# One stage for the sample rows' delta rule, paged attention and head gate, with the heads' split moved into the MLP stage

## What is computed

```
proj = rmsnorm(x) @ w_in
o_g  = gated delta rule(q, k, v, g, beta, S0)      # 4 heads, state S of 128 x 128 per head and sequence
o_g  = rmsnorm(o_g) * silu(z)                      # per head
o_d  = (softmax(q1 k1) - lam * softmax(q2 k2)) @ v # 4 heads; samples read 512 past keys and values from pages
o_d  = rmsnorm(o_d) * (1 - lam_init)
h    = x + concat(o_g, o_d) @ w_out
y    = h + (silu(u_gate) * u_value) @ w_down,  u = causal conv(rmsnorm(h) @ w_up)
```

## Time and profile before

| | us |
|---|---|
| median of 3 runs | 1882.63 (1879.61 to 1882.79) |
| the profiled execution | 1877.6 |
| its span, first to last instruction | 1876.0 |
| stages one and two of the span | 780.9 |
| `delta_sample` | 62.6 |
| `attention_sample` | 71.9 |
| `head_gate` | 66.6 |
| `output_and_mlp` | 894.0 |

### The profile page before, as it was taken

One profiled execution on the slowest core, in us unless ns is written; L12 is line 12 of the kernel. 1 busy time (PEld: TensorE's weight loads), 2 busy tenths in 40 slices (PEclk: granted clock), 3 DMA queues, 4 the chain that ended last, 5 costly groups with the idle time before them and its releaser, 6 DMA issues. The chain is left out here.

```text
span 1876.0 us, 28466 instructions
## 1 busy us (share of the span) xinstructions
PE 1722.7 (92%) x11078; PEld 1615.1 (86%) x11078; DVE 1007.0 (54%) x1450; ACT 536.0 (29%) x803; POOL 247.1 (13%) x434
## 2 busy tenths in 40 slices
PE   5999999997999999765559999999999999999998
PEld 5999998895888888644139999999999999999997
DVE  4444388673556665332163455555655655655654
ACT  4243323321434443201232223212212212212213
POOL 3100022214333333104000000000000000000000
PEclk9999999997999999857769999999999999999999
DMA  4311111221000000119302121101101101101103
GB/s 142 119 45 48 45 36 42 84 81 35 1 12 1 12 1 1 51 45 359 140 10 66 48 68 57 57 22 56 56 22 56 56 22 56 56 22 56 55 0 102
DMA packets 114550, 105.29 MB, mean 56 GB/s; under 512 B 5387, under 2 KB 104221, under 8 KB 112022
## 3 DMA queue, kind: packets, MB, share of 16 engines
q1 hardware_dynamic: 111666, 93.35, 16.0%
q0 software_dynamic: 1536, 8.39, 1.1%
q10 hardware_dynamic: 1270, 2.48, 0.4%
HBM read 86.13 MB, written 18.07 MB: 56 GB/s over the span
## 5 line engine op out<-in xcount | busy, mean ns | idle before, releaser
L2656 PE MATMUL f_up<-h_hi,w_hi 128*128 128x352 f32 x1032 | 335.1, 325 | 1.9 <-DVE w_lo L2465 1.2
L2656 PE MATMUL f_up<-h_hi,w_lo 128*128 128x352 f32 x1032 | 333.4, 323 | 0.0
L2656 PE MATMUL f_up<-h_lo,w_hi 128*128 128x352 f32 x1032 | 333.4, 323 | 0.0
L179 PE MATMUL proj<-x_hi,win_hi 128*128 128x352 f32 x672 | 227.4, 338 | 5.3 <-issue 3.0
L179 PE MATMUL proj<-x_hi,win_lo 128*128 128x352 f32 x672 | 217.5, 324 | 0.0
L179 PE MATMUL proj<-x_lo,win_hi 128*128 128x352 f32 x672 | 217.3, 323 | 0.0
L2656 PEld LDWEIGHTS f_up<-h_hi,w_hi 128*128 128x128 f32 x1032 | 193.8, 188 | 2.5 <-DVE w_lo L2465 1.5
L2656 PEld LDWEIGHTS f_up<-h_hi,w_lo 128*128 128x128 f32 x1032 | 194.1, 188 | 0.0
L2656 PEld LDWEIGHTS f_up<-h_lo,w_hi 128*128 128x128 f32 x1032 | 193.7, 188 | 0.0
L2663 PE MATMUL f_down<-f_g_hi,dn_hi 128*128 128x352 f32 x512 | 165.4, 323 | 0.0
L2663 PE MATMUL f_down<-f_g_hi,dn_lo 128*128 128x352 f32 x512 | 164.7, 322 | 0.0
(11 more groups left out here) (405 smaller groups left out, 3033.9 us busy)
## 6 DMA issues: line engine op xcount, KB each, us to landing
w_raw<-in_w_up SPq DMA_DIRECT2D x44, 512.0 KB, 3.9
win_raw<-in_w_in SPq DMA_DIRECT2D x28, 512.0 KB, 4.0
dn_raw<-in_w_down SPq DMA_DIRECT2D x11, 1024.0 KB, 5.1
p_key<-in_cache_k SPq DMA_DIRECT2D x32, 256.0 KB, 6.4
p_val<-in_cache_v POOLq DMA_DIRECT2D x32, 256.0 KB, 6.2
x_scratch<-feat SPq DMA_DIRECT2D x1, 4224.0 KB, 13.4
feat<-x_scratch SPq DMA_DIRECT2D x1, 4224.0 KB, 17.4
feat<-in_x_prompt SPq DMA_DIRECT2D x8, 512.0 KB, 8.4
```

What stands on the lines that cost most here:

```text
L179: mm = nc.tensor.matmul(out, w[:, k, :], x[:, k, g * TG:(g + 1) * TG], start=(k == 0 and i == 0), stop=(k == KT - 1 and i == 2))
L2656: mm = nc.tensor.matmul(up[u % RING][:, 0:TG], a[s][:, kk, :], b, start=(kk + x == 0), stop=(kk == KT - 1 and x == 2))
```

## The change

The three stages become one, `sample_stage`, with one barrier where there were three.

- The delta rule's steps are laid between the steps of the key loop. PE's order in the loop is: `delta_join(0)`, turn 1, `delta_extend(0)`, score 0; `delta_join(1)`, turn 2, `delta_extend(1)`, score 1; `delta_solve`, turn 3, `delta_state` (the 64 matmuls), score 2; the new values, turn 4, the output, score 3; then in b = 4 and b = 5 four state updates each, two ahead of the turn and two behind it; then b = 6 and 7 as before.
- The transposed keys go through two banks in place of four, one head each: ACT keeps heads 0 and 2, DVE heads 1 and 3. The other banks are `bank_a` and `bank_b` (delta rule, state updates, later the sums of squares), two for scores and two for the fresh part; the score and key banks also serve the first delta steps.
- The state update is cut into eight halves of one 512-column matmul each. The decay of the state moves from DVE to POOL, four instructions behind POOL's value loads.
- Values of sequences 0 to 3, 6 and 7 lie in tiles of `feat`. Those of 6 and 7 take the place of 0 and 1, and are loaded only when `multiply(0)` is done.
- z is read on SP's queue behind the keys of b = 2, silu is applied by ACT at b = 5. The sums of squares go group by group: `sum_heads(0)` behind the loop, `sum_heads(1)` behind `turn_map(1)` and `turn_out(0)`, `sum_heads(2)` behind `multiply(1)`. Roots, reciprocals and spreading work on one column group at a time (and a small fourth group of the 32 sample columns); the spread results use the two key banks in turn. The multiplication with silu(z) moves to POOL.
- The split of the heads into `o_hi` and `o_lo` moves into `output_and_mlp`, ahead of and around the split of the first weights. x is read there as well (8 DMAs on SP's queue, behind the first two weight loads). The first output tile is computed with the heads in the outer loop and the three column groups in the inner one.

The diff, cut to its core (NV is 6 and SB is 4; in the MLP stage DVE has the same order with `o_low` and `low` as ACT with `o_high` and `high`):

```diff
-    phase(delta_sample, i, o, c, feat, ba)
-    phase(attention_sample, i, o, c, feat)
-    hT = feat[:, H:3 * H, :]
+    phase(sample_stage, i, o, c, feat, ba, z_scratch)
...
-    phase(head_gate, c, hT, feat, o_hi, o_lo, x_scratch, z_scratch)
-    phase(output_and_mlp, i, o, c, feat, hT, o_hi, o_lo, o_at, feat_at)
+    phase(output_and_mlp, i, o, c, feat, o_hi, o_lo, o_at, feat_at, x_scratch)
...
+    bank_a, bank_b = m.ps("s_bank_a", [P, 512]), m.ps("s_bank_b", [P, 512])
+    key_ps = [m.ps(f"p_key_ps{x}", [P, 512]) for x in range(2)]
...
         def _(sp):
+            sp.dma_start(state[:, :, :], i["state_gdn_S"][0].rearrange("b h k v -> k (b h) v")).then_inc(state_in, 16)
             for b in range(NB):
                 if b >= NK:
-                    sp.wait_ge(key_turned[1], b - NK + 1)
+                    sp.wait_ge(key_turned[1], 2 * (b - NK + 1))
...
+                if b == 2:
+                    sp.dma_start(zT, z_scratch[:, :, 0:SEQ]).then_inc(z_in, 16)
+                    sp.dma_start(z_few[:, :, :], z_scratch[:, :, SEQ:T]).then_inc(z_few_in, 16)
+            sp.wait_ge(dve_done, DV["S7"])
+            sp.dma_start(o["gdn_S_sample"][0].rearrange("b h k v -> k (b h) v"), state[:, :, :]).then_inc(state_out, 16)
...
         @block.gpsimd
         def _(pool):
...
+            for b in range(NV):
+                load_values(b)
+            pool.wait_ge(state_in, 16)
+            pool.wait_ge(pe_done, PE["wqS"])
+            for h in range(H):
+                mine = state[:, :, :].rearrange("p (b h) v -> p b h v", h=H)[:, :, h, :]
+                last = e_row[:, h, :].rearrange("p (b l) -> p b l", b=NB)[:, :, NL - 1:NL]
+                nc.gpsimd.tensor_tensor(mine, mine, last.to_broadcast([P, NB, DH]), ALU.mult).then_inc(decayed, 1)
+            pool.wait_ge(multiplied, 1)
+            for b in range(NV, NB):
+                load_values(b)
+            pool.wait_ge(z_made, H)
+            for g in range(NG):
+                for t in range(H):
+                    pool.wait_ge(normed, NH * g + t + 1)
+                    x = head_out[t][:, GROUPS[g]]
+                    nc.gpsimd.tensor_tensor(x, x, zT[:, t, GROUPS[g]], ALU.mult).then_inc(gated, 1)
...
             def turn_keys(b):
...
+                for h in range(H):
+                    if 2 * b + h // 2 >= 1:
+                        pe.wait_ge(key_kept[h % 2], 2 * b + h // 2)
+                    for j in range(NPG):
+                        mm = nc.tensor.transpose(key_ps[h % 2][:, j * PAGE:(j + 1) * PAGE], key_in[s][:, j, h * DH:(h + 1) * DH],
+                                                 c["ident"][:, :])
+                    mm.then_inc(key_turned[h % 2], 1)
...
+            sum_heads(0)
             turn_map(1)
             turn_out(0)
+            sum_heads(1)
             multiply(1)
+            sum_heads(2)
             turn_out(1)
+            for g in range(NG):
+                for t in range(NH):
+                    spread_roots(g, t)
+                if g == 1:
+                    sum_heads(NG)
+            for t in range(NH):
+                spread_roots(NG, t)
...
+                if b == SB + 1:
+                    act.wait_ge(z_in, 16)
+                    for t in range(H):
+                        nc.scalar.activation(zT[:, t, :], zT[:, t, :], ACT.Silu).then_inc(z_made, 1)
...
+            for t in range(3):
+                o_high(t)
             high(0, 0)
+            for t in range(3, KT):
+                o_high(t)
             high(1, 1)
...
+            for k in range(KT):
+                pe.wait_ge(o_lo_done, k + 1)
+                for g in range(NG):
+                    at = slice(g * TG, (g + 1) * TG)
+                    for x, (a, b) in enumerate(((w_hi, o_hi), (w_hi, o_lo), (w_lo, o_hi))):
+                        mm = nc.tensor.matmul(up[g][:, 0:TG], a[0][:, k, :], b[:, k, at], start=(k + x == 0), stop=(k == KT - 1 and x == 2))
```

More of the change, by code:

```diff
@@ L909, in norm_and_projection @@
     m.free()
[L912 to L994, removed]
-                                        ).then_inc(lo_done, 1)
-    def spread(pe, t, psum):
-        for g in range(NG):
-            if t == 0:
-                pe.wait_ge(lo_done, g + 2)
-            for k, part in enumerate((hi, lo)):
-                mm = nc.tensor.matmul(psum[:, g, 0:TG], spread_r[:, t, :], part[:, g * TG:(g + 1) * TG], start=(k == 0), stop=(k == 1))
-        return mm
-    return on_pool, on_scalar, on_tensor, on_vector, spread
@@ new lines, in _ @@
+            square(0, 2)
+            square(0, 3)
+            exps(1)
+            for t in range(4, NH):
+                square(0, t)
+            keep_out(0)
+            nc.scalar.preload_act_table(ACT.Sqrt)
+            act.wait_ge(strip_zero, 2)
+            root(0)
+            for t in range(NH):
+                square(1, t)
+                if t == 4:
+                    high(0)
+            root(1)
+            keep_out(1)
+            for t in range(NH):
+                square(2, t)
+                if t == 4:
+                    high(1)
@@ L2147, in _ @@
             keep_map(1)
+            invert(0)
+            low(0)
             add_rows(0)
+            invert(1)
+            low(1)
+            for t in range(4):
+                norm(0, t)
             add_rows(1)
+            for t in range(4, NH):
+                norm(0, t)
+            invert(2)
+            low(2)
+            for t in range(NH):
+                norm(1, t)
+            for t in range(4):
+                norm(2, t)
+            invert(NG)
+            for t in range(4, NH):
+                norm(2, t)
@@ new lines, in _ @@
+            low(NG)
+            dve.wait_ge(spread_done, NH * NG + 1)
+            for x in range(2):
+                rows = feat[:, 3 * H * x:3 * H * x + H, SEQ:T]
+                nc.vector.scalar_tensor_tensor(out=rows, in0=rows, scalar=c["gain"][:, x:x + 1], in1=cols(bank_a, x, P),
+                                               op0=ALU.mult, op1=ALU.mult).then_inc(normed, 1)
+            dve.wait_ge(z_made, H + 1)
+            dve.wait_ge(normed, NH * NG + 1)
+            rows = feat[:, 0:H, SEQ:T]
```

766 lines of the change are left out of this document (466 added, 300 removed).

## The result

The changed kernel takes 1838.07 us in the median of four runs (1832.0 to 1844.06), the kernel before 1881.66 (1879.61 to 1882.79): ratio 0.9778 with a 95% interval of 0.9758 to 0.9798, 43.6 us less. The forecast was 1836.8.

What follows compares the result with a forecast made beforehand. Outside PE's MLP stage, hand-over chains, DMA and 1.2 GHz PE work bound the kernel. Removing 46.9 us at a cost of 1.1 takes the profiled 1877.6 to 1831.8; 5.0 for the median gives 1836.8, range 1814 to 1862 (own range 1826 to 1850).

Steps and rivals of the forecast that it cites:

- First turn: Start of the key loop: state and first keys landed at 793, early delta steps done by then at no cost.
- Turn of b = 3: Key loop: z ahead on SP's queue delays these keys to 820, not 809; PE idle from about 812.
- State matmuls: Key loop, behind turn 3: 64 matmuls take 13.8 us at the low clock, done at 838.7.
- The rest of the key loop: After the state matmuls: 36 us of PE at mixed clocks plus 4 of hand-overs, ending at 879.
- The silu: ACT at b = 5: near 8 us ahead of the keys of b = 7, beside 4 to 8 of PE work.
- From the loop's end to the stage's: Sums, multiply(1) and spreading behind the key loop: from 879 to 934.3, barrier to 935.1; spreads 0.75 us apart.
- MLP stage: Stage after the merged one: PE's first matmul comes 1.1 us later, behind ACT's casts and DVE's subtractions; cost 1.1.
- B: Key loop: keys of b = 3 pass at about 811 and the rest runs near 2.4 GHz; 1817, chance 0.17.
- C: Merged stage: PE stays at 1.2 GHz, loop +16, sums +10, multiply(1) +2; 1865 us, chance 0.22.
- D: Merged stage: two banks in turn don't overlap, 80 hand-overs cost 0.8 us more each; 1901 us, chance 0.05.
- The rule left out of the sum: Spreads of vn beside POOL's decays: two to four would wait up to 2.4 us each, 5 to 10 worse.

Runs made afterwards that it cites:

- e2: The changed kernel with z read behind the keys of b = 4 in place of b = 2: 1824.4 us, ratio 0.9702.
- e1: The changed kernel run again without any edit, as yardstick: 1841.0 us, ratio 0.9781.
- e5: The changed kernel with POOL's four state decays also waiting for VectorE's second spread of the new values: 1837.5 us, ratio 0.9777.
- e8: The changed kernel with all eight state updates through one PSUM bank in place of two in turn: 1845.8 us, ratio 0.9821.
- e6: The changed kernel with both operands of the eight state updates zero-padded from 32 to 128 rows: 1833.8 us, ratio 0.9757.
- e9: The changed kernel with the state matmuls ahead of the turn of b = 3 and ScalarE's silu of z taken during them: 1822.6 us, ratio 0.9701.
- e10: The same as e9, plus updates and root spreads zero-padded to 128 rows: 1815.8 us, ratio 0.9660.
- e3: The changed kernel with the 64 state matmuls ahead of the turn of b = 3, z kept in place: 1825.1 us, ratio 0.9714.
- e11: The same as e3, plus updates and root spreads zero-padded to 128 rows, silu left in place: 1821.0 us, ratio 0.9687.
- e4: The changed kernel with all delta-rule steps ahead of the key loop, stages still merged: 1836.3 us, ratio 0.9776.

## Why the prediction was right, and where it was not

The time was met within 1.3 us, but in part by luck, because errors cancel. The forecast for the profiled execution was a stage of 154.2 us; it took 165.7. Each step, from the stage's start, with the forecast beside it:

- First turn: 12.7 us (12.1). The early delta steps cost nothing, as said.
- Turn of b = 3: 45.6 (39.1), **+6.5**. The mechanism, the queue served in order with z ahead of the keys, was right, and e2 shows it; its size was not. The step took two queues at their full rates from 793 on. In the trace 273 GB/s moved from 783 to 800 and 396 from 800 to 820, not 418 throughout. That the order on the queue counts, and not only the bytes, follows from e2: z's 2.1 MB are 5 us at 418 GB/s, and the turn came 10.2 us earlier than in e1.
- State matmuls: 13.82 (13.8). With turn and copies 17.7 (18.7), **-1.0**. In e5 to e8, with the same state matmuls in the same place, they took 11.0 to 11.3, since a part of them ran at the high clock; so this row isn't one value either.
- The rest of the key loop: 49.6 (40.3), **+9.3**. This is the term that was furthest off. The forecast took a mixture of clocks, 36 us of PE between 28 and 54, and 4 of hand-overs. PE was busy for 47.0, since its clock was 0.50 in all of 857.8 to 885.6, and waited for 2.6, of which 2.44 are VectorE's beside POOL: the hand-overs were not the error. e6 and the pair e9 and e10 show what the clock hung on in part: with the updates padded to 128 rows it is 0.95 over six of them in e6, and 0.94 in e10 where e9 has 0.74. Without padding the term isn't one value either: 44.1 us in e5, 44.7 in e3, 49.5 in e1.
- The silu: hidden, as forecast, but only while the loop is slow: with the padding PE waits 3.02 us for it in e6 and 3.01 in e11.
- From the loop's end to the stage's: 52.8 (56.1), **-3.3**. All of it lies before the spreads, which start 25.2 us behind the loop's end (29 forecast): `multiply(1)` starts at 908.7, and values didn't hold it. The spreads themselves came 0.65 apart at 1.00 and 0.81 at 0.50 where 0.75 was said.
- MLP stage: +0.6 (+1.1). Its first matmul comes 7.27 us after the stage's first DMA (7.4), by the chain that was named: 

```profile
947.96 1.28 ACT L2527
949.25 1.08 ACT o_hi L2536
...
950.36 3.60 DVE o_lo L2659 x3
953.95 1.15 DVE w_lo L2628
...
955.14 4.92 PE f_up L2799 x19
```

The four steps in bold make +11.5 for the stage; with -0.5 in the MLP stage (+0.6 for +1.1) and 1.3 us in the stages ahead, which the change doesn't touch, the profiled run lies 12.3 us over the 1831.8 forecast for it. What set the time right again was the step from one profile to the median. The forecast added 5.0 us to its span because before's profiled run lay that far under its median; the changed kernel's profiled run lay 6.0 over its own. Against the median the stage was less far off. With the 1670.1 to 1675.9 us that the profiled runs spend outside of it, a run of 1838.1 has a stage of 162 to 168 us to the first MLP matmul; that is an estimate. The forecast had 161.6, the profiled run 172.9, and e5, a run of 1836.0, 163.9. So the forecast was low by up to 6 us for a middle run, and the 5.0 us that it added for before's profile made up for most of that.

Two sums of the forecast don't come out. From its own bounds for the loop's end (867 and 897 around 879) its range is 1825 to 1855 and not 1826 to 1850, and B's 1836.8 - 19 is 1817.8. Neither changes the reading of the result.

**The rivals.** B (1817) held a clock and a queue that were not so in this kernel; its two halves came true with e2 or e3 and with e10 (1815.8), by edits. C (1865) was near on the loop's clock and wrong on its cause and on the rest: 0.50 in 857.8 to 885.6, but 1.00 in the sums (895.1 to 924.5). Its page, TensorE: Matmul & The Clock Gate of the Trainium skill, section Part 4: PE-mode transpose, has transposes not bring the full clock; e4's key loop of transposes and scores ran at 0.94, so here transposes with scores among them did not hold the clock down. Padding the updates among them raised it. D (banks in turn don't overlap) is refuted for the updates by e8: if they did not, one bank would have cost nothing, and PE waits 3.5 us for it; for the turned keys by the trace, where the 16 transposes of b = 5 and of b = 6 take 3.87 us without a wait, and took 3.67 with four banks.

**The rule left out of the sum.** The Trainium skill, page SBUF — State Buffer, section Who interferes with whom, has a VectorE instruction with two SBUF inputs and a GpSimd instruction that reads SBUF exclude each other. The trace agrees: one of eight spreads took 2386 ns beside the decays, the others 669, and in e4 one took 5.43 us. It also costs POOL something: a decay takes 1.90 us alone and up to 2.35 where it meets a spread. The price, 5 to 10 us in the forecast, was too high: two spreads fell beside the decays, but the second followed the first at its usual length, and PE waited 2.44.

## What to carry to other kernels

Where stages are merged, look first at what the merged queue puts ahead of the first thing that PE waits for, and give PE the work that needs no load; that was 13 to 17 us here, from either of two small edits. Small matmuls between large ones are not only their own length: read the granted clock over the stretch, and if it is 0.50 while PE is fully busy, try zero rows up to 128, which cost PE nothing here (2.08 us against 2.07 for an update); with the wait for the silu out of the way both paddings were worth 6.8 us. And after any gain look for what was hidden with little to spare (here the silu), because the next gain ends there.

## What the runs showed of the hardware that was not expected

- The same program on the same chip takes 1834.7 to 1846.3 us, in step with its mean granted clock of 0.963 to 0.954. The 64 state matmuls took 13.82 us in both profiles of the changed kernel and 11.0 to 11.3 in e5 to e8, where they are unchanged.
- A key loop with PE busy 27.8 of 27.8 us ran at 0.50, one with PE busy 25.85 of 33.6 at 0.94. Being busy is not what told them apart; zero rows added to eight updates raised the clock (0.50 to 0.95 in e6, 0.74 to 0.94 from e9 to e10). The last four updates ran at the high clock in all three padded traces (e6, e10, e11) and, but for some in e8, at the low one in all others. But 32 rows did not always bring it down: the first four updates of e3 and e9 ran at the high clock (1.02 to 1.12 us), and single ones in e8 (1.12 us at 860.71). So this is a tendency with a cause that isn't settled: whether it is the rows, or the updates' share in the stretch, no run here tells.
- A VectorE instruction of 0.67 us lasted 5.43 in e4, until POOL's last decay was through, behind most of three in a row. It isn't always held to their end: in e5 a spread took 1.30 us and was done at 854.7, with POOL's decays going on to 856.4.
